# Where the modulation product's work lies: from the first merge and output product to the second attention

## What is computed

```python
x = first_block(x, ...)                   # nsa attention, merge with gates, output product
c_act = silu(c)
mod = c_act @ w_ada + b_ada               # 2048 x 12288
sh1, sc1, g1, sh2, sc2, g2 = split(mod, 6)
h = rms_norm(x, norm1_w) * (1 + sc1) + sh1
proj = h @ w_in                           # q, k, v of both attentions, gates ga and gb
ya = global_gqa(...)                      # grouped-query: 8 heads, 2 keys and values
yb = neighbourhood_attention(..., rpb)    # 8 heads with a bias
merged = sigmoid(ga) * (ya @ w_oa) + sigmoid(gb) * (yb @ w_ob)
x = x + g1 * (merged @ w_out)
h2 = rms_norm(x, norm2_w) * (1 + sc2) + sh2
x = x + g2 * ((silu(h2 @ w_gate) * (h2 @ w_up)) @ w_down)
return rms_norm(x, final_w)
```

## Time and profile before

| | us |
|---|---|
| median of three runs | 2336.08 |
| lowest and highest of them | 2335.11, 2340.84 |
| the profiled execution | 2335.34 |
| its span, first to last instruction | 2333.7 |
| PE busy | 2270.6 |
| DVE busy | 1554.9 |
| ACT busy | 1099.7 |
| mean granted TensorE clock | 0.995 |

### The profile page before, as it was taken

The page is one execution under the profiler, slowest core; times in us unless marked ns, Lnnn a source line. Parts: engine busy times, 40 slices in busy tenths (PEclk is TensorE's granted clock), DMA queues, the critical chain, the costliest instruction groups (busy, mean ns, idle before and its releaser), DMA issues. The chain is left out here.

```text
span 2333.7 us, 31287 instructions
## 1 busy us (share of the span) xinstructions
PE 2270.6 (97%) x10377; PEld 1866.3 (80%) x10377; DVE 1554.9 (67%) x1937; ACT 1099.7 (47%) x1429; POOL 149.7 (6%) x285
## 2 busy tenths in 40 slices
PE   8999999999999998899999999998999999999997
PEld 6888888778778787788877888887888888888885
DVE  5675777776775887778754556656556666665557
ACT  6554445565554343433355564444444443444443
POOL 1000110000001211010000100000000000000000
PEclk9999999999999999999999999999999999999999
DMA  8787896555566998677555656764666666666563
GB/s 286 278 298 254 323 333 226 207 188 190 196 236 203 356 377 315 223 281 278 196 171 171 208 187 228 247 231 162 216 219 225 227 227 226 225 215 213 200 207 120
DMA packets 150104, 546.49 MB, mean 234 GB/s; under 512 B 17249, under 2 KB 17392, under 8 KB 148496
## 3 DMA queue, kind: packets, MB, share of 16 engines
q1 hardware_dynamic: 112976, 407.42, 50.4%
q0 software_dynamic: 34752, 129.71, 16.0%
q10 hardware_dynamic: 2304, 8.39, 0.9%
HBM read 534.92 MB, written 10.53 MB: 234 GB/s over the span
## 5 line engine op out<-in xcount | busy, mean ns | idle before, releaser
L1012 DVE TENSOR_TENSOR w_lo<-raw,w_hi 128x1024 fp32r<-128x1024 f32 x769 | 936.0, 1224 | 662.7 <-ACT w_hi L598 650.3
L598 ACT ACTIVATE w_hi<-raw 128x1024 fp32r<-128x1024 f32 x769 | 812.6, 1060 | 1048.6 <-PE ps L1733 828.0
L1731 PE MATMUL ps<-w_hi,a_hi 128*128 128x512 f32 x1632 | 640.5, 392 | 15.1 <-DVE w_lo L1012 8.0
L1733 PE MATMUL ps<-w_hi,a_lo 128*128 128x512 f32 x1632 | 637.7, 391 | 0.0
L1732 PE MATMUL ps<-w_lo,a_hi 128*128 128x512 f32 x1632 | 637.4, 391 | 0.0
L1731 PEld LDWEIGHTS ps<-w_hi,a_hi 128*128 128x128 f32 x1632 | 307.9, 189 | 80.4 <-DVE w_lo L1012 6.7
L1733 PEld LDWEIGHTS ps<-w_hi,a_lo 128*128 128x128 f32 x1632 | 307.8, 189 | 64.5
L1732 PEld LDWEIGHTS ps<-w_lo,a_hi 128*128 128x128 f32 x1632 | 307.9, 189 | 63.1
L1847 PE MATMUL ps<-w_hi,a_hi 128*128 128x512 f32 x640 | 259.1, 405 | 5.3 <-ACT gst L686 5.3
L1849 PE MATMUL ps<-w_hi,a_lo 128*128 128x512 f32 x640 | 250.3, 391 | 0.0
L1848 PE MATMUL ps<-w_lo,a_hi 128*128 128x512 f32 x640 | 250.1, 391 | 0.0
(11 more groups left out here) (292 smaller groups left out, 2050.4 us busy)
## 6 DMA issues: line engine op xcount, KB each, us to landing
raw<-ws_dram SPq DMA_DIRECT2D x769, 512.0 KB, 4.2
ada<-wa_dram POOLq DMA_DIRECT2D x192, 512.0 KB, 4.9
gates_spill<-gst ACTq DMA_DIRECT2D x16, 512.0 KB, 3.4
ga<-gates_spill POOLq DMA_DIRECT2D x8, 512.0 KB, 4.5
gb<-gates_spill POOLq DMA_DIRECT2D x8, 512.0 KB, 6.7
bias_c<-b_merge_dram POOLq DMA_DIRECT2D x9, 256.0 KB, 5.2
x<-x_dram SPq DMA_DIRECT2D x4, 512.0 KB, 7.5
cb<-c_dram POOLq DMA_DIRECT2D x2, 1024.0 KB, 7.4
```

The costliest lines, as they stand in the source:

```text
L598: act.activation(w_hi[:, k.slot(RING), :], raw[:, k.slot(RING), :], ACT.Copy).then_inc(hi_done, 1)
L1012: dve.tensor_tensor(w_lo[:, k.slot(RING), :], raw[:, k.slot(RING), :], w_hi[:, k.slot(RING), :].bitcast(F32), ALU.subtract).then_inc(lo_do ...
L1731: pe.matmul(o, hi(m, tb), w_hi[:, s, cols], start=m == 0, stop=False)
L1733: mm = pe.matmul(o, lo(m, tb), w_hi[:, s, cols], start=False, stop=m == of * kts - 1)
```

## The change

It moves 52 modulations, 36 of merge1 and 16 of out1, into the second attention, 13 per group. They have two buffers there, `ada2`, and semaphores of their own; what lay in that memory (`kT2`, `gst2`) gets other places. DVE does one behind a filling tile (`fill_late`) and one behind a unit's maximum. The sums of rows 2 to 4 are formed behind the last group, and turned and copied inside merge2's first chunk. POOL deals the loads of the pieces, the bias and the gates in a new order. And `gqa.fill` has its third and fourth number changed.

```diff
-ADA_TURN = {"proj": (6, 4), "qup": (12, 3), "nsa": (6, 4), "merge1": (18, 2), "out1": (16, 1), "proj2": (12, 2),
+ADA_TURN = {"proj": (6, 4), "qup": (12, 3), "nsa": (6, 4), "proj2": (12, 2), "gates2": (13, 4),
             "ff": (4, 8)}
...
-        kT2 = at("kT2", ADA, [P, 4, S])
-        gst2 = at("gst2", ADA + 12 * K, [P, TB, NC])
...
-        ada2 = at("ada2", R + 56 * K, [P, 2, TW])
+        ada2 = at("ada2", ADA, [P, 2, TW])
+        ada3 = at("ada3", R + 56 * K, [P, 2, TW])
...
+        kT2 = at("kT2", SC + 20 * K, [P, 4, S])
+        gst2 = at("gst2", R + 36 * K, [P, TB, NC])
...
-        gqa.fill = (1, 2, 4, 5, 4)
+        gqa.fill = (1, 2, 5, 4, 4)
...
             for c in range(4):
                 gates_load(0, c, c + 1)
...
-                for k in range(n):
-                    load_ada(At(ADA0["merge1"] + ADA_RING + n * c + k))
...
+            def load_late(m0, m1):
+                for m in range(m0, min(m1, ADA0["ff"] - ADA0["gates2"])):
+                    if m >= 2:
+                        pool.wait_ge(ada2_used, m - 1)
+                    pool.dma_start(ada2[:, m % 2, :], wa[ADA0["gates2"] + m]).then_inc(ada2_landed[m % 2], 16)
...
+            n = ADA_TURN["gates2"][0]
+            pool.wait_ge(ada_used, ADA0["gates2"])
+            load_late(0, 2)
+            load_bias(0)
+            load_late(2, 2 * n + 2)
+            for g in (2, 3):
+                load_late(n * g + 2, n * g + 5)
+                load_bias(2 * g - 3)
+                load_late(n * g + 5, n * g + 9)
+                if g == 2:
+                    load_bias(2)
+                load_late(n * g + 9, n * g + n + 2)
+            pool.wait_ge(na.qk_done, len(na.units) * na.groups)
+            gates_load(1, 0, 5)
             pool.wait_ge(gates_out, 16 * 17)
-            for c in range(1, 4):
-                gates_load(1, c, 4 + c + 1)
+            gates_load(1, 1, 6)
             rows_store(2, 2, 5)
             pool.wait_ge(rows_out, 32)
             pool.wait_ge(na.y_done, TB * na.groups + 1)
             pool.dma_start(g12[:, 0], row(2)).then_inc(g_in, 16)
+            for c in range(2, 4):
+                gates_load(1, c, 4 + c + 1)
...
+                def fill_late(n, m, turns_):
+                    for x in range(n):
+                        fill(1)
+                        if x < turns_:
+                            modulation2(ada0 + (m + x), m + x, ada2, cb)
+
+                if nsa_:
+                    fill(a.fill[1])
                 else:
-                    fill(a.fill[0])
-                fill(a.fill[1])
+                    fill_late(a.fill[0] + a.fill[1], 0, 3)
...
+                        else:
+                            modulation2(ada0 + (3 + 4 * j), 3 + 4 * j, ada2, cb)
 
                         dve.wait_ge(a.exp_done, (u + 1 + 1).n)
...
-                    fill(a.fill[2 + j])
+                    if nsa_:
+                        fill(a.fill[2 + j])
+                    else:
+                        fill_late(a.fill[2 + j], 4 + 4 * j - j // nu, 3 if j < nu else 2)
...
-                    steps(At(k), 4, a0, 3, m0)
+                    steps(At(k), 4)
                     merged_lo("merged1", 2 * c - 2)
...
-                    steps(At(k), RING, a0 + m0, m1 - m0, m0)
+                    steps(At(k), RING)
...
             for n, a in enumerate((gqa, gqa, na, na)):
-                attention(a, n % 2, At(n % 2), At(T0["gates2"] + 2 * T_K * n))
-                if n == 0:
-                    modulation_sums(2 * KT, 5 * KT)
...
+                attention(a, n % 2, At(n % 2), At(T0["gates2"] + 2 * T_K * n),
+                          At(ADA_TURN["gates2"][0] * n), At(KEPT0["gates2"] + n))
+            modulation_sums(2 * KT, 5 * KT)
...
                 if c == 0:
+                    rows_turn(2, 2 * KT, 5 * KT)
                     pe.wait_ge(na.y_done, len(na.units) * na.groups + 1)
```

More of the change, by code:

```diff
@@ L511, in _ @@
             pool.wait_ge(gates_out, 16 * 9)
-            n = ADA_TURN["merge1"][0] // 2
             for c in range(4):
@@ L533, in _ @@
             pool.dma_start(shift1_b[:], row(0)).then_inc(shift_rows, 16)
-            n = ADA0["ff"] // ADA_RING
-            with pool.Fori((ADA0["out1"] + ADA_RING) // ADA_RING, n) as i:
+            n = ADA0["gates2"] // ADA_RING
+            with pool.Fori((ADA0["proj2"] + ADA_RING) // ADA_RING, n) as i:
                 for k in range(ADA_RING):
                     load_ada(At(k, ADA_RING, i))
-            for k in range(n * ADA_RING, ADA0["ff"]):
-                load_ada(At(k))
-            pool.wait_ge(mod_ready, 2)
@@ new lines, in load_bias @@
+            def load_bias(u):
+                if u:
+                    pool.wait_ge(bias_used, u)
+                g, tb = u // TB, u % TB
+                for half in range(2):
+                    tr = 2 * tb + half
+                    for h in range(4):
+                        pool.dma_start(
+                            na_bias[64 * half:64 * half + 64, h, :],
+                            t["rpb"][4 * g + h, :, (ROWS - 1 - tr) * GRID_W:(2 * ROWS - 1 - tr) * GRID_W])\
+                            .then_inc(bias_in, 16)
@@ L944, in _ @@
                 if c == 0:
-                    steps(At(k), 2 * T_H)
+                    steps(At(k), T_H)
+                    rows_copy(2, 3 * KT)
+                    steps(At(k + T_H), T_H)
                 else:
@@ L1023, in modulation, with modulation2 @@
                     .then_inc(ada_used, 1)
+            def modulation2(k, m, tiles, c):
+                dve.wait_ge(ada2_landed[k.slot(2)], k.lap(2, 16))
+                a, half = tiles[:, k.slot(2), :], k.base % 2
+                dve.tensor_tensor_reduce(out=a, in0=a, in1=c[:, half * TW:(half + 1) * TW], scale=1.0, scalar=0.0,
+                                         op0=ALU.mult, op1=ALU.add, accum_out=mod_part[:, m:m + 1])\
+                    .then_inc(ada2_used, 1)
             def keep_modulation(a, n, kept):
@@ L1175, in attention @@
                     keep_modulation(ada0, n_ada, kept)
+                else:
+                    n = ADA_TURN["gates2"][0]
+                    c0 = ADA0["gates2"] + ada0.base
+                    dve.wait_ge(ada2_used, ada0.n + n)
+                    dve.tensor_copy(mod2[:, c0:c0 + n], mod_part[:, 0:n]).then_inc(mod_kept, 1)
+                    dve.wait_ge(mod_kept, kept.n + 1)
             for a in (nsa, gqa, na):
@@ L1313, in _ @@
                         chain.on(dve.tensor_tensor(gp, gp, both(scale_b[:, h]), ALU.mult))
-                    steps(At(k + 2), 2, a0, 3, m0)
+                    steps(At(k + 2), 2)
                     dve.wait_ge(dve_chain, chain.n)
@@ L1325, in _ @@
                     pool_lo(3)
[L1326 removed]
+                    steps(At(k + 7), 1)
                 else:
[L1328 removed]
+                    steps(At(k), 4)
                     merged_lo("merged1", 2 * c - 2)
@@ L1454, in _ @@
                 if c < 3:
-                    steps(At(k + RING), T_K - RING, a0 + m1, m2 - m1, m1)
+                    steps(At(k + RING), T_K - RING)
                     if c == 0:
```

58 lines of the change are left out of this document (12 added, 46 removed).

## The result

| us | before | after | predicted |
|---|---|---|---|
| median of the runs | 2335.6 (four runs, 2332.96 to 2340.84) | 2315.7 (four runs, 2313.11 to 2318.65) | 2318.7 |
| ratio, 95% interval | | 0.9912 [0.989, 0.9935] | |
| the profiled execution | 2335.34 | 2318.65 | 2318.0 |
| its span | 2333.7 | 2317.0 | |

The account below looks back on a forecast made before the run. TensorE, busy 97% of the span, was taken as the bound. Gains 8.8 + 2.5 + 7.05 = 18.3 us, carrying 1.0: 2335.3 - 18.3 + 1.0 = 2318.0, or 2318.7 on the median's scale; range 2314 to 2328.

Parts of the forecast that it names:

- Place a: First chunk of the output product: a late modulation load leaves a 6.27 us TensorE gap, then half clock; gain 8.8 us.
- Place b: First merge: a modulation waits 4.91 us for its transfer beside other loads, causing gaps of 2.02 and 0.49; gain 2.5 us.
- Place c: Grouped-query attention: the new fill puts ScalarE's gate eviction ahead of the exponentials; gain 5.35 us plus 1.7 of clock, 7.05.
- The carrying: Second attention: cost of taking 52 modulations with two buffers at 4.8 us landing; 1 us lost, ends 0 and 8.
- The Trainium skill's 3.2 us: Second attention: estimated landing of a 512 KB load, 2.0 us plus bytes at 436 GB/s; the sum used 4.8 instead.
- Other moved steps: Second merge's gates, row store and g row, transposed rows, modulation sums: nothing lost; sums 1 us without their cover.
- 2: Rival at the gate chunk: the stall stays because ScalarE stands behind in another way; 2326 us, chance 0.06.
- 1: Rival in the second attention: data late, not fatal, landing about 6.4 to 7; 5 to 10 us lost, 2323 to 2328, chance 0.15.
- rival 3: Two buffers bound all four attentions: at landing 8, 30 us lost, 2348; gain eaten from 7.5; chance 0.04.
- 4: Rival in the second attention: VectorE's own work holds up POOL's loads, landing 7.2 us; 9.4 us beyond forecast, 2328, chance 0.02.
- 5: Rival at a or b: another POOL load lands last in the modulation's place; at most 2.5 us back, 2321, chance 0.03.
- The floating stretch: Slow clock after norm2's gaps may go or come, a like one may come after norm3: 1.7 us either way.

Follow-up runs that it names:

- the experiment with the x rows: Kernel before, with the x row loads (2 MB) moved from the second to the last chunk of the first merge, all modulations in place; 2337.6 us.

## Why the prediction was right, and where its terms were off

The direction, the size and the mechanism of all three places came out: 2315.7 against 2318.7 in the medians. That the profiled executions agree to 0.65 us, 2318.65 against 2318.0, is luck: the profile happens to be of the slowest of four runs. Of its steps:

- **Place a, 8.8 us.** Right: 8.9 in the stage, of which moving the loads alone brings 8.1. The clock's part was right too, the stage runs at 1.00 in after. In other executions of before the place costs about 1 us less.
- **Place b, 2.5 us.** 3.1 in the stage: the two gaps are gone, and 0.6 us in steps too short for the list of gaps. In two other executions of that merge it was 2.0 and 2.3. Its cause, the shared transfers, is shown by the experiment with the x rows; so is that not every way of parting them wins, since a later x load stalls VectorE for 9.4 us.
- **Place c, 7.05 us.** Right as a size when done alone, 7.4. Its working was incomplete: it compared the deal with the old VectorE order. The step that says "gain 5.35 us" took the edit as independent of the move; with the modulations and the old deal, the gaps would have been 6.5 and 6.9 us. The forecast was not hurt by this, since both were in the change, but anyone who had read "7 for the deal, 11 for the move" from it would have expected the move alone to give 11, and it gives 2 in the medians (2334.0 against 2336.0), which the runs can't tell from nothing.
- **The carrying, 1 us.** The mis-sized term: 2.8 us, inside its ends of 0 and 8. The landing was taken as 4.8 us and measured 5.2 in the median, at 298 GB/s where 310 was estimated; by the median the two buffers keep up, (1.5 + 5.2)/2 = 3.35 under 4.17. What failed is the step from the mean to the single place: the hand count gave every load the same landing and started from a full slack in every group, while single loads took up to 9.2 us and VectorE waited 19 times, up to 3.3 us.
- **The Trainium skill's 3.2 us.** By the estimate from the Trainium skill (DMA: Bandwidth & Descriptors, Anatomy of one DMA) no modulation would have waited. Here 19 waited: the stage's shortest landing, 3.3 us, is near that estimate, the median of 5.2 is not. The measurement decides.
- **"Other moved steps", nothing.** Right: no wait at the gates of merge2, at the row store or at the sums; the merge starts without a gap.
- **The rivals.** 2 is out (no gst wait over 0.2 us). 1 is there in kind, at the size of 2.8 and not 5 to 10. 3 was brought about by halving the loads in flight, +87 us. 4 has the landings above against it. In rival 3 the loss at L = 7.5 is 4 x 4.3 by its own working (4.5 us times 13, less 54.2), not 4 x 4.6; it changes no bound. 5 didn't happen: no load takes the place of the modulations at a or b.
- **The floating stretch.** Announced for 1.7 us either way, and it did come up: in after it is behind norm3, not norm2: 1.6 us won and 1.1 lost.

The sum was closer than its parts, and that is luck: 1.8 us too little for the carrying, and 0.6 lost ahead of the first merge where nothing was changed, stand against 0.6 at b, 0.4 at c, 0.1 at a and 0.5 from the clock.

## What to carry to other kernels

Work on a second engine can be moved to wherever that engine has time, but it is in front of something there: ask of each moved piece which later instruction of the same engine it stands ahead of, and who waits for that one. Two edits that touch the same chain are to be valued together, since one may cover what the other exposes; here the move without the deal was worth 2 us, the deal without the move 8, both 20. And a ring whose mean rate is enough still loses where several loads in a row land late: one more buffer costs 4 KB per partition and took that loss from 2.8 us to nothing.

## What the runs showed of the hardware

The same gap doesn't always cost the clock. Behind norm2 and norm3 TensorE stands 2.74 or 2.75 us in the profiles of all the kernels here, and what the clock does then differs, even between two executions of one kernel. With three buffers, in the first series behind norm2:

```profile
977.00:980.00 3.00, 3.00 (x9) 2.35 (x8) 0.73 (x1) 0.00 (x0) 0.00 (x0) 0.51 0.76 243
```

In the second, the same kernel at the same place:

```profile
977.00:980.00 3.00, 3.00 (x17) 2.48 (x16) 0.76 (x1) 0.00 (x0) 0.00 (x0) 1.00 0.80 223
```

Nine matmuls at the 1.2 GHz level in the first, seventeen at 2.4 GHz in the second. The span of the first is 2313.5 us, of the second 2311.8. From norm2 to the first scores the first takes 196.88 us, the second 195.29. So 1.6 us of difference between two profiled executions may be nothing but this, and terms of that size are to be read from a stage that has no such gap.

The median landing of the pieces in the second attention went with the number of their buffers: 3.6 us with one load in flight, 5.2 with two, 5.5 and 5.7 with three (up to 12.1). The traffic of the stage went up along with it (226 GB/s with one, 298 with two), so these runs don't part the two causes. With the third buffer the single load was no faster, and the waits for the data were nearly gone.
